# Attention stage of a two-block model: ScalarE's PSUM evictions placed ahead of its exponentials, VectorE's reciprocals placed one step later

## The reference, cut to what matters

```
# sliding window attention with sinks, 8 heads, window 128, per block of 128 queries
s  = q @ k.T / 8 + bias;  m = max(s.max(-1), sink);  e = exp(s - m)
pr = e / (e.sum(-1) + exp(sink - m));  o_a = pr @ v
# latent attention over the selected keys, 8 heads, per block of 128 queries
s  = q_abs @ c_kv.T / 8 + bias, NEG where a key was not selected
pr = softmax(s);  lat = pr @ c_kv;  o_b = lat @ w_uv
```

## Time and profile before

| | |
|---|---|
| time, median of 3 executions | 3791.87 us (3783.33 to 3792.92) |
| the profiled execution, its own time | 3794.53 us |
| span of the profile | 3792.8 us |
| mean granted TensorE clock of the profile | 0.957 |
| attention stage | about 2436 to 2808 us of the span |
| PE busy over the whole span | 3517.5 us (93%) |
| DVE, ACT, POOL busy | 45%, 29%, 12% |

### The profile page before, as it was taken

One profiled execution on the slowest core, in us unless ns is written; L12 is line 12 of the kernel. 1 busy time (PEld: TensorE's weight loads), 2 busy tenths in 40 slices (PEclk: granted clock), 3 DMA queues, 4 the chain that ended last, 5 costly groups with the idle time before them and its releaser, 6 DMA issues.

```text
span 3792.8 us, 46132 instructions
## 1 busy us (share of the span) xinstructions
PE 3517.5 (93%) x19094; PEld 2536.7 (67%) x19094; DVE 1708.1 (45%) x3339; ACT 1103.0 (29%) x2242; POOL 446.4 (12%) x746
## 2 busy tenths in 40 slices
PE   8899999999999899999878899888889999999998
PEld 7775876777677577577453344567764478888886
DVE  3433444344343435435417889655532233332424
ACT  3432342243243333133212111355531131111112
POOL 0110120011021423022510011100000000000000
PEclk9899999999999999999978999999999999999999
DMA  3010110100001010011010022100031011111111
GB/s 132 23 35 9 42 40 1 39 29 23 28 29 40 12 42 29 28 40 70 1 70 34 22 81 72 48 1 1 1 131 42 12 52 49 45 56 45 54 47 45
DMA packets 36524, 151.52 MB, mean 40 GB/s; under 512 B 4983, under 2 KB 9785, under 8 KB 28890
## 3 DMA queue, kind: packets, MB, share of 16 engines
q1 hardware_dynamic: 36314, 148.57, 11.3%
HBM read 132.82 MB, written 15.73 MB: 39 GB/s over the span
## 4 chain that ended last, share of the span: by engine, by line
PE 82%; DVE 8%; ACT 4%; POOL 3%; issue 2%; DMA 1%; SPq 0%; POOLq 0%; DVEq 0%; ACTq 0%
PE pp L559 7%; PE pp L561 7%; PE pp L560 6%; PE pp L1210 6%; PE pp L1211 6%; PE pp L1212 6%; PE pp L1045 6%; PE pp L725 5%; PE pp L1192 3%; PE pp L1176 2%; PE pp L870 2%; PE pp L1140 2%; PE pp L1035 2%; PE pp L1124 1%; PE pp L917 1%
## 5 line engine op out<-in xcount | busy, mean ns | idle before, releaser
L559 PE MATMUL pp<-gx_hi,pw_hi 128*128 128x512 f32 x1168 | 486.6, 417 | 28.5 <-DVE pw_lo L1787 27.7
L561 PE MATMUL pp<-gx_hi,pw_lo 128*128 128x512 f32 x1168 | 466.1, 399 | 0.0
L560 PE MATMUL pp<-gx_lo,pw_hi 128*128 128x512 f32 x1168 | 465.9, 399 | 0.0
L559 PEld LDWEIGHTS pp<-gx_hi,pw_hi 128*128 128x128 f32 x1168 | 226.5, 194 | 77.3 <-DVE pw_lo L1787 30.4
L1210 PE MATMUL pp<-x_hi,wt_hi 128*128 128x512 f32 x704 | 274.4, 390 | 1.1 <-DVE x_lo L2328 1.1
L1212 PE MATMUL pp<-x_hi,wt_lo 128*128 128x512 f32 x704 | 273.9, 389 | 0.0
L1211 PE MATMUL pp<-x_lo,wt_hi 128*128 128x512 f32 x704 | 273.9, 389 | 0.0
L561 PEld LDWEIGHTS pp<-gx_hi,pw_lo 128*128 128x128 f32 x1168 | 225.5, 193 | 50.1
L560 PEld LDWEIGHTS pp<-gx_lo,pw_hi 128*128 128x128 f32 x1168 | 226.9, 194 | 44.0
L725 PE MATMUL pp<-xT,arena 128*128 128x512 f32 x512 | 233.8, 593 | 6.3 <-DVE arena L1961 6.3
L1787 DVE TENSOR_TENSOR pw_lo<-arena,pw_hi 128x1024 fp32r<-128x1024 f32 x73 | 89.6, 1228 | 243.4 <-ACT pw_hi L1265 243.3
(11 more groups left out here) (390 smaller groups left out, 6588.1 us busy)
## 6 DMA issues: line engine op xcount, KB each, us to landing
arena<-in_tiles_dram SPq DMA_DIRECT2D x73, 512.0 KB, 3.6
arena<-in_units_dram SPq DMA_DIRECT2D x33, 1024.0 KB, 5.0
xT<-in_w_outs_dram SPq DMA_DIRECT2D x6, 2048.0 KB, 8.1
xT<-in_wall_dram SPq DMA_DIRECT2D x6, 2048.0 KB, 7.9
w<-in_wall_dram SPq DMA_DIRECT2D x4, 2048.0 KB, 8.3
gates_scratch<-arena SPq DMA_DIRECT2D x32, 256.0 KB, 2.4
arena<-gates_scratch SPq DMA_DIRECT2D x8, 1024.0 KB, 4.8
arena<-in_xT_dram SPq DMA_DIRECT2D x8, 512.0 KB, 8.0
```

The source lines that it names most:

```text
L559: mm(b[:, hs], wh[:, c], X[0][:, k, hs], k == 0, False)
L560: mm(b[:, hs], wh[:, c], X[1][:, k, hs], False, False)
L561: m = mm(b[:, hs], wl[:, c], X[0][:, k, hs], False, k == 7)
```

## The change

The order of the callbacks inside a step is altered in attend_order, and the window attention's ACT callback gets a name and a place of its own. PE's queue stays exactly as it is. In ACT's queue the exponential of the latent row and, behind it, the window exponentials move to a place behind the copies of swa_turn(m - 1) and swa_out(m - 2); they still come ahead of the copies of queries and absorbed. In DVE's queue the reciprocal of unit k moves from step k + 1 to step k + 2, still at the head of the step. Nothing is added or removed, no size is changed, no buffer and no DMA is touched.

```
-        def attend_order(queries, absorbed, scale, scores, latent, turn_p, raised, turn_o, expo, swa_scores, swa_turn, swa_scale,
-                         swa_values, swa_out):
+        def attend_order(queries, absorbed, scale, scores, latent, turn_p, raised, turn_o, expo, swa_scores, swa_expo, swa_turn,
+                         swa_scale, swa_values, swa_out):
...
-                if 1 <= s_ < 65:
-                    scale(s_ - 1)
+                if 2 <= s_ < 66:
+                    scale(s_ - 2)
...
-                if s_ < 64:
-                    expo(s_)
                 m = s_ // 2
                 if s_ % 2 == 0:
                     if m < 32:
...
                         swa_scale(m)
                     if 1 <= m < 33:
                         swa_values(m - 1)
+                if s_ < 64:
+                    expo(s_)
+                    if s_ % 2 == 0:
+                        swa_expo(m)
                 for later, at_ in ((2, 8), (3, 13)):
...
-            def swa_scores(m):
+            def swa_expo(m):
                 i, j, d, cs, k0, ln, bo = swa_keys(m)
```

More of the change, by code:

```diff
@@ L1154, in turn_o @@
                 q.then_inc(*did("ot", k))
-            attend_order(queries, absorbed, skip, scores, latent, turn_p, raised, turn_o, skip, swa_scores, swa_turn, skip,
-                         swa_values, swa_out)
+            attend_order(queries, absorbed, skip, scores, latent, turn_p, raised, turn_o, skip, swa_scores, skip, swa_turn,
+                         skip, swa_values, swa_out)
             def did(*event):
@@ L1698, in turn_o @@
                     ).then_inc(*did("oT", k))
-            attend_order(queries, absorbed, skip, skip, latent, turn_p, raised, turn_o, expo, swa_scores, swa_turn, skip, skip,
+            attend_order(queries, absorbed, skip, skip, latent, turn_p, raised, turn_o, expo, skip, swa_expo, swa_turn, skip, skip,
                          swa_out)
@@ L2290, in scale @@
                 e.reciprocal(rd, sm_).then_inc(*did("rd", k))
-            attend_order(skip, skip, scale, scores, skip, skip, skip, skip, skip, swa_scores, skip, swa_scale, swa_values, skip)
+            attend_order(skip, skip, scale, scores, skip, skip, skip, skip, skip, swa_scores, skip, skip, swa_scale,
+                         swa_values, skip)
             def did(*event):
```

## The result

The changed kernel takes **3735.93 us** (median of 4; 3732.46 to 3742.49) against 3789.18 for the kernel before in the same series (median of 4). The ratio is **0.9863, 95% interval 0.9843 to 0.9883**: 53 us faster. Run once more on another occasion it gave 3739.69 and a ratio of 0.9868 (0.9853 to 0.9882). The profiled execution took 3742.49 us with a span of 3740.8, against 3794.53 and 3792.8.

What follows compares the result with a forecast made beforehand. PE was taken to bound the attention stage, with 49 us idle and a clock of 0.95 to win from. Waits 29.6 + clock 13 = 42.6 us off 3794.5 gives 3752, 3750 against the median; range 3739 to 3772.

Steps and rivals of the forecast that it cites:

- The bound and the cause: Attention stage: PE busy 331 of 380 us; 40.3 us of its idle time end with ACT's copy of swa_turn.
- a new wait of 0.44 us: Third-quarter pairs with swa_out: raised waits for ACT's copy of latent, ACT's chain 3.35 us against PE's 2.91, replacing 2.20.
- No gain: Twelve pairs without swa_out: waits 4.3 us before and 4.3 after, raised waiting for the window exponentials by another path.
- the sum of the waits: PE's waits in the attention stage: gains of 21.8 + 4.8 + 3.0 = 29.6 us, bounds 22 to 34.
- pairs with swa_out, with absorbed, with queries: Gains in PE's waits: 21.8 us in twelve pairs with swa_out, 4.8 in three with absorbed, 3.0 in three with queries.
- PE's own path: PE's work from swa_turn's end until raised, pairs with swa_out: estimated 2.69, 2.79, 2.91, 3.01 us by quarter.
- The clock: Seven falls after the stage's start, 31 us at 1.2 GHz, loss up to 15.5; six vanish, gaining 13 us.
- The rule of the Trainium skill: Frequent small idles between matmul groups can make PE's clock swing; by it the gain would be 29.6 us instead of 42.6.
- The reciprocals: DVE's 64 reciprocals a step later: costed at nothing; without the move a 0.4 us delay in an odd step, mostly hidden.
- DVE waiting long for the exponentials: Attention stage, listed as a sign that the forecast is wrong; no size given.
- The rivals: Clock keeps falling, 3762 us, 0.14; new wait larger, about 3777, 0.13; slower, 3805, 0.04; does nothing, 3792, 0.06.
- Slower: Raised behind ACT's chain: a chain 1.8 us longer than counted loses about 13 us, 3805 us; chance 0.04.

Runs made afterwards that it cites:

- the trebled copy: Changed kernel with ACT's copy of the long row's latent made three times in each odd step; 3752.20 us, ratio 0.9902.

## Why the prediction was right, and where it was wrong

**The bound and the cause.** Right. PE was the bound, the window exponentials with ScalarE's wait for VectorE were what delayed the copy of swa_turn, and taking them out of its way is worth all of the gain; the run with only them moved shows that the long exponential's move adds nothing.

**The step that failed** is this one: "Then raised needs the copy of latent. So a new wait of 0.44 us appears, before line 1147 for line 1686". In a step, latent works on unit s_ - 3 and raised on unit s_ - 4. Raised reads a latent that was copied in the step before. The first instruction that needs this step's copy is the next but one in the two-bank ring, swa_values or turn_o, as the trebled copy shows. PE so has the 0.17 us of raised as extra cover in every pair. It has this in the twelve pairs without swa_out too, where raised waits for neither path any more and where I wrote "No gain". ScalarE's chain is as I summed it: 3.28 us from 2630.51 to 2633.79 in the pair shown, against 3.35.

What became of the sum of the waits, with 0.15 us of tail for each as there:

| | before | after, forecast | after, measured |
|---|---|---|---|
| pairs with swa_out, with absorbed, with queries | 39.9 | 10.3 | 3.3 idle (1.4 + 1.3 + 0.2 + 0.4) in 8 waits, 4.5 with tails |
| pairs without swa_out | 4.3 | 4.3 | 1.1 idle in 4 waits, 1.7 |

So the waits gave 38 us and not 29.6. The step above is less than half of these 8.4 us: 0.17 us off each forecast slip (0.10 off the smallest four) is 3.8 us. Two more terms were mis-sized.

- **PE's own path** from the end of swa_turn to raised, in the pairs with swa_out and without absorbed. I summed 2.69, 2.79, 2.91, 3.01 us for the four quarters; the timelines have 3.18, 3.07, 2.95, 3.18. In the first quarter, for instance, the two matmuls of the short scores take 0.41 us where 0.0017 a column made 0.24, and latent waits 0.22 us for the copy of swa_turn, for which I had put nothing there. PE arrives later by itself, so the copy of latent, at 3.5 to 3.2 us as summed, delays it by at most 0.16 us. By an estimate from these figures that is 2 to 3 us of the 8.4.
- **The pairs without swa_out.** From the start of the short scores to swa_values takes 3.53 us in eleven of these twelve pairs before (2.87 in the first), and 3.04 in the first and then 3.23, 3.12, 3.02 and mostly 3.14 us, by quarter, after. They gave 4.4 us, more than the 2.6 that the idle times of the table show. In the last quarter neither profile has a wait there, and yet each pair is 0.3 to 0.4 us shorter: delays below the tail are in no wait. The split between the table's two rows is therefore rough; their sum is borne out by the latent span.

The waits before swa_values for the copy of raised stayed, as forecast: 2.0 us, 2.4 before.

**The clock.** The mechanism was right, the size a little small: I counted six of seven falls, all seven went. By the windows of the earlier trace rows they are 30.6 us at 1.2 GHz, 15.3 us of loss, where I put 13. The added transposes show this part alone: the latent span fell by 14.2 us. 38 + 15.3 = 53 us; the latent span fell by 52.6. What decides whether a fall follows stays open: of the fifteen waits of 1.9 to 2.9 us in the kernel before, seven were followed by one and eight were not, where my text named only two without.

After the change 28 idle times of 0.2 to 0.8 us remain in the stage, and the granted clock is 1.00. The rule of the Trainium skill that I weighed there (TensorE: Matmul & The Clock Gate, "A second HAM failure mode: psum-queue depth-cycling", on frequent small idles) would have left the clock swinging; this trace does not agree with it.

**The reciprocals.** Costed at nothing, and worth nothing: 1.0003 by themselves, and the same time without them. I had argued that the delay without the move would be 0.4 us in an odd step and mostly hidden. It is up to 1.2 us, 15.2 in all, and no part of it shows in the latent span. "DVE waiting long for the exponentials", which I had named as a sign of being wrong, comes without any cost.

**The range.** Its lower end took waits of 34 us as the bound, from an uncertainty in ScalarE's chain alone. It didn't ask whether the instruction that I had named as the one that waits was the right one. Bounding the new waits by nothing from below would have given 44 + 15.5, and the range would have held the time. **The rivals** were all for smaller gains; none came. "Slower" named the right resource, ScalarE's chain up to the copy of latent, and the run with only the long exponential moved is a kernel for which it holds: there ScalarE's idle time doubles and the chain decides.

## What to carry to other kernels

When an engine in strict order both frees buffers and does work that waits for a third engine, put the freeing first: here a copy of half a microsecond started 2.6 us late, behind exponentials of other units and a wait for their input. Before pricing the wait that comes next, write down for each instruction of a pipelined step which unit it works on; one step of lag decides who waits. And add what idle time costs in clock to what it costs by itself: of the 53 us about 38 were waiting and 15 were matmuls at half speed behind the waits.

## What the runs showed of the hardware that I had not expected

Useless work made the kernel faster: 256 added transposes, 28 us of TensorE time, put into fifteen idle times of 1.9 to 2.9 us and one place without any, took 13 us off the total (0.9969, 0.9959 to 0.9978), as TensorE's granted clock stayed at its 2.4 GHz level. The falls are not tied to one place: in the kernel before and in the run with only the reciprocals moved, PE's waits on line 1647 are the same to 0.1 us, yet the first has 31 us at 1.2 GHz after the start of the stage and the second 34, and waits of 2.4 us that are followed by a fall in the second are not in the first. The fall at the start of the stage, 6.8 us long, is in every kernel.
